# Second feed-forward stage: gate and up of two token blocks by seven half-depth products, the third block in a pass of its own

## The reference, cut to what matters

```python
def _rmsnorm(x, g):
    y = xf * lax.rsqrt(jnp.mean(xf * xf, axis=-1, keepdims=True) + EPS)
    return (y * g).astype(x.dtype)

def _swiglu(x, w_gate, w_up, w_down):
    return (jax.nn.silu(x @ w_gate) * (x @ w_up)) @ w_down

x = x + 0.5 * _swiglu(_rmsnorm(x, ffn1_norm[l]), ffn1_w_gate[l], ffn1_w_up[l], ffn1_w_down[l])
y, ... = _mixer(_rmsnorm(x, mix_norm[l]), ...)      # convolution and mLSTM, output projection
x = x + y
x = x + 0.5 * _swiglu(_rmsnorm(x, ffn2_norm[l]), ffn2_w_gate[l], ffn2_w_up[l], ffn2_w_down[l])
return _rmsnorm(x, final_norm)
```

## Time and profile before

| | us |
|---|---|
| median of 3 runs | 1892.54 |
| lowest, highest | 1892.49, 1892.79 |
| the profiled execution | 1891.52 |
| its span on the chip | 1889.8 |
| TensorE busy in the span | 1869.8 |
| VectorE busy | 881.0 |
| ScalarE busy | 498.2 |
| GpSimd busy | 97.7 |

### The profile page before, as it was taken

One profiled execution on the slowest core, in us unless ns is written; L12 is line 12 of the kernel. 1 busy time (PEld: TensorE's weight loads), 2 busy tenths in 40 slices (PEclk: granted clock), 3 DMA queues, 4 the chain that ended last, 5 costly groups with the idle time before them and its releaser, 6 DMA issues.

```text
span 1889.8 us, 31119 instructions
## 1 busy us (share of the span) xinstructions
PE 1869.8 (99%) x12577; PEld 1855.6 (98%) x12577; DVE 881.0 (47%) x1536; ACT 498.2 (26%) x883; POOL 97.7 (5%) x156
## 2 busy tenths in 40 slices
PE   8999999999999999999999999999999999999998
PEld 8999999999999999999999999999999999999998
DVE  6524433443444338513688865534434443343344
ACT  5302211221122124334444633212211221122022
POOL 1000000000000013200110022000000000000001
PEclk9999999999999999999999999999999999999999
DMA  7012201220121012311111322012201210220102
GB/s 226 26 43 67 67 22 44 67 67 22 44 67 52 14 54 73 82 45 45 35 34 41 132 81 68 23 46 67 67 22 44 67 50 16 67 67 23 55 1 92
DMA packets 144178, 105.10 MB, mean 56 GB/s; under 512 B 6376, under 2 KB 136248, under 8 KB 144120
## 3 DMA queue, kind: packets, MB, share of 16 engines
q1 hardware_dynamic: 144032, 104.27, 18.0%
q10 hardware_dynamic: 88, 0.02, 0.0%
HBM read 95.36 MB, written 8.92 MB: 55 GB/s over the span
## 4 chain that ended last, share of the span: by engine, by line
PE 94%; DVE 4%; ACT 1%; issue 0%; DMA 0%; POOL 0%; DVEq 0%
PE bank L218 30%; PE bank L224 29%; PE bank L223 29%; PE bank L222 1%; PE bank L220 1%; PE bank L678 1%; PE bank L2105 0%; PE bank L2119 0%; PE bank L2118 0%; PE bank L2121 0%; PE bank L685 0%; PE bank L941 0%; ACT in_hi L1209 0%; PE bank L2148 0%; DVE ffn_normed L194 0%
## 5 line engine op out<-in xcount | busy, mean ns | idle before, releaser
L218 PE MATMUL bank<-in_hi,w_hi 128*128 128x352 f32 x2256 | 712.9, 316 | 3.4 <-DVE w_lo L1109 1.6
L223 PE MATMUL bank<-in_lo,w_hi 128*128 128x352 f32 x2256 | 705.0, 313 | 0.0
L224 PE MATMUL bank<-in_hi,w_lo 128*128 128x352 f32 x2256 | 705.0, 313 | 0.0
L218 PEld LDWEIGHTS bank<-in_hi,w_hi 128*128 128x128 f32 x2256 | 426.4, 189 | 6.7 <-issue 2.2
L223 PEld LDWEIGHTS bank<-in_lo,w_hi 128*128 128x128 f32 x2256 | 426.5, 189 | 1.2
L224 PEld LDWEIGHTS bank<-in_hi,w_lo 128*128 128x128 f32 x2256 | 426.4, 189 | 0.0
L423 DVE TENSOR_TENSOR ffn_hidden<-ffn_silu,bank 128x352 f32<-128x352 f32 x132 | 68.7, 521 | 595.8 <-PE bank L224 528.9
L218 PE MATMUL bank<-ffn_hidden_hi,ffn_w_hi_more 128*128 128x352 f32 x1056 | 331.0, 313 | 1.0 <-DVE x L434 1.0
L434 DVE SCALAR_TENSOR_TENSOR x<-bank,x 128x352 f32<-128x352 f32 x528 | 261.1, 524 | 127.3 <-PE bank L224 92.3
L223 PE MATMUL bank<-ffn_hidden_lo,ffn_w_hi_more 128*128 128x352 f32 x924 | 288.8, 313 | 0.0
L224 PE MATMUL bank<-ffn_hidden_hi,ffn_w_lo_more 128*128 128x352 f32 x924 | 288.8, 313 | 0.0
(11 more groups left out here) (224 smaller groups left out, 1480.9 us busy)
## 6 DMA issues: line engine op xcount, KB each, us to landing
raw<-in_ffn_w_gate SPq DMA_DIRECT2D x44, 512.0 KB, 4.0
ffn_raw_more<-in_ffn_w_down SPq DMA_DIRECT2D x44, 512.0 KB, 5.3
raw<-in_w_in SPq DMA_DIRECT2D x24, 512.0 KB, 3.9
raw<-in_ffn_w_up SPq DMA_DIRECT2D x22, 512.0 KB, 5.0
ffn_raw_more<-in_ffn_w_up SPq DMA_DIRECT2D x22, 512.0 KB, 5.3
x_parked<-x SPq DMA_DIRECT2D x3, 1408.0 KB, 5.6
x<-x_parked SPq DMA_DIRECT2D x3, 1408.0 KB, 10.8
raw<-in_w_out SPq DMA_DIRECT2D x8, 512.0 KB, 4.9
```

What stands on the lines that cost most here:

```text
L218: pe.matmul(out, w_hi, in_hi, start=first, stop=False)
L223: pe.matmul(out, w_hi, in_lo, start=False, stop=False)
L224: return pe.matmul(out, w_lo, in_hi, start=False, stop=last)
```

## The change

The hidden stage is taken out of `ffn_phase` for the second feed-forward and rewritten as `last_ffn_phase`:

- Blocks 0 and 1 are done first, for all 11 pairs. The first two pairs are done as before (four plain rounds). For the nine pairs after that, gate and up of two tiles and two blocks are one product of 2x2 half matrices (two output tiles by two halves of the depth, and two halves of the depth by two blocks), made from seven products of half depth (12 matmuls each: four parts of 128, three products) instead of eight. Sums and differences of weight halves (t) are made on VectorE from the raw tiles and split on ScalarE and VectorE; sums and differences of the inputs (s1 to s4) are made once, in the plain rounds and behind them. The results are summed on VectorE while further products accumulate in the same banks. Down is done as before, for two blocks in one go, 96 matmuls.
- Block 2 has its place in `in_hi`/`in_lo` taken by s1 and s2 in the meantime. Its norm split is made at the end of the ninth such pair, and it goes through the 11 pairs alone in a third pass, for which all weight tiles are loaded and split a second time. The down tiles are loaded into the raw buffers of gate.
- The final norm's transposes of tiles 0 to 4 stand in the last three rounds; its output buffers are nine, each used once.
- The two feed-forward stages share the weight semaphores, so the counts of the second have an offset `base`.

The core of the diff:

```diff
+PRODUCTS = ("x11", "s2", "s1", "s3", "x12", "x22", "s4")
+DOWN_RAW = {**SLOT, ("down", 0): SLOT["gate", 0], ("down", 1): SLOT["gate", 1]}
+    # SyncE
+        def pair_loads(pair, number, seven, next_tile, last):
+            if not (isinstance(number, int) and number == 0):
+                sp.wait_ge(f.low["gate"], number * 2 + (base * 2 + 2))
+                if seven:
+                    sp.wait_ge(q.t_made, kind_index(pair, "gate") * 4 + 4)
+                load("down", pair, DOWN_RAW)
...
+                sp.wait_ge(f.low["down"], number * 2 + (base * 2 + 2))
...
+            load("gate", next_tile, SLOT)
+            sp.wait_ge(f.low["up"], number * 2 + (base * 2 + 2))
+            if seven:
+                sp.wait_ge(q.t_made, kind_index(pair, "up") * 4 + 4)
+            load("up", next_tile, SLOT)
+    # VectorE: sums of the inputs
+        def sums(k, n):
...
+            whole(f0, x21)
+            whole(f1, inputs["x22"][k])
+            step_op(f1, f0, f1, ALU.add)
+            whole(f0, inputs["x11"][k])
+            step_op(f2, f1, f0, ALU.subtract)
+            whole(f3, inputs["x12"][k])
+            step_op(f3, f3, f2, ALU.subtract)
+            s_low("s1", k, f1, n)
+            s_low("s2", k, f2, n + 1)
+            s_low("s4", k, f3, n + 2)
+        def third_sums():
+            for k in range(HALF):
+                whole(f0, (sh.in_hi[:, k, block_columns(1)], sh.in_lo[:, k, block_columns(1)]))
+                whole(f2, inputs["x11"][k])
+                step_op(f2, f2, f0, ALU.subtract)
+                s_low("s3", k, f2, 12 + k)
+    # VectorE: the plain rounds
+                hidden_of(step, 0, silu_four)
...
+                if (pair, b) == (0, 1):
+                    sums(0, 0)
+                if (pair, b) == (1, 0):
+                    sums(2, 6)
+                if b:
+                    weight_low(dve, sh, f, "gate", 0, pair + 1)
+                    weight_low(dve, sh, f, "up", 0, pair + 1)
+                hidden_of(step, 1, silu_four)
...
+                for d in range(4, KT):
+                    add(r * 8, b, d, down_bank)
+                    if (pair, b) == (1, 1) and d == 4:
+                        t_low(0, 0)
+                        t_make("gate", 1, 0)
+                if (pair, b) == (0, 1):
+                    sums(1, 3)
+                if (pair, b) == (1, 0):
+                    sums(3, 9)
+                if (pair, b) == (1, 1):
+                    t_low(2, 0)
+                    t_low(1, 0)
+                    t_make("gate", 3, 0)
+                    third_sums()
+    # VectorE: a pair of the seven products
+            a16("gate", kg, silu_four)
+            t_low(3, kg)
+            t_make("up", 0, ku)
+            t_make("up", 2, ku)
+            weight_low(dve, sh, f, "down", 0, pair, DOWN_RAW)
+            weight_low(dve, sh, f, "down", 1, pair, DOWN_RAW)
+            both22("gate", kg, silu_four)
+            t_low(0, ku)
+            t_make("up", 1, ku)
+            t_low(2, ku)
+            c21("gate", kg, silu_four)
+            t_low(1, ku)
+            t_make("up", 3, ku)
+            c12("gate", kg, silu_four)
+            a16("up", ku, hidden)
+            t_low(3, ku)
+            weight_low(dve, sh, f, "gate", 0, pair + 1)
+            weight_low(dve, sh, f, "gate", 1, pair + 1)
+            if not last:
+                t_make("gate", 0, ku + 1)
+                t_make("gate", 2, ku + 1)
+            both22("up", ku, hidden)
+            hidden_make(0)
+            if not last:
+                t_low(0, ku + 1)
+            hidden_make(1)
+            low(0)
+            if not last:
+                t_make("gate", 1, ku + 1)
+                t_low(2, ku + 1)
+            low(1)
+            c21("up", ku, hidden)
+            hidden_make(2)
+            low(2)
+            c12("up", ku, hidden)
+            hidden_make(3)
+            if not last:
+                t_low(1, ku + 1)
+            low(3)
+            if not last:
+                t_make("gate", 3, ku + 1)
+            own_adds_done(pair * 16)
...
+            if last:
+                weight_low(dve, sh, f, "up", 0, pair + 1)
+                adds(range(2))
+                weight_low(dve, sh, f, "up", 1, pair + 1)
+                adds(range(2, 4))
+                norm_split_dve(dve, sh, own_norm, gain, lambda k: adds(range(4 + k, 5 + k)))
+                adds(range(12, 16))
+            else:
+                adds(range(4))
+                weight_low(dve, sh, f, "up", 0, pair + 1)
+                adds(range(4, 6))
+                weight_low(dve, sh, f, "up", 1, pair + 1)
+                adds(range(6, 16))
+    # TensorE: a pair of the seven products
+                for name in PRODUCTS:
+                    if name == "s2":
+                        pe.wait_ge(q.t_low, kind * 4 + T_SPLIT[1])
+                        if w == "gate":
+                            pe.wait_ge(s.x_added, count - 1)
+                            if first:
+                                pe.wait_ge(q.s_step, S_EARLY_STEPS)
+                    if name == "s1" and w == "gate":
+                        pe.wait_ge(s.x_added, count)
+                    if name == "s3":
+                        if first and w == "gate":
+                            pe.wait_ge(q.s_step, S_STEPS)
+                        pe.wait_ge(q.summed, kind * 5 + 1)
+                    if name == "x12":
+                        pe.wait_ge(q.first_copied, kind + 1)
+                    if name == "x22":
+                        pe.wait_ge(q.summed, kind * 5 + 2)
+                        pe.wait_ge(q.t_low, kind * 4 + 4)
+                    if name == "s4":
+                        pe.wait_ge(q.summed, kind * 5 + 3)
...
+            drain(down(count, tiles, ((1, 0), (0, 2)), seven_down, pair, True))
+            drain(down(count + KT, tiles, ((0, 1), (1, 3)), seven_down, pair, False))
+    # third pass, VectorE
+            for j in range(2):
+                weight_low(dve, sh, f, "down", j, number, DOWN_RAW)
+            hidden_of(step, 0, last_silu)
+            tail.scales(dve, tiles)
+            if not last:
+                weight_low(dve, sh, f, "gate", 0, number + 1)
+                weight_low(dve, sh, f, "up", 0, number + 1)
+            hidden_of(step, 1, last_silu)
```

More of the change, by code:

```diff
@@ L210, in norm_split_act, with products @@
                        ).then_inc(sh.norm_high, 1)
-def products(pe, out, w_hi, w_lo, in_hi, in_lo, first=True, last=True, low_ready=None):
+def products(pe, out, w_hi, w_lo, in_hi, in_lo, first=True, last=True, low_ready=None, resumed=False):
     in_hi, in_lo = streamed(in_hi), streamed(in_lo)
+    if resumed:
+        pe.matmul(out, w_hi, in_hi, start=False, stop=False, skip_group_check=True)
+        pe.matmul(out, w_hi, in_lo, start=False, stop=False, skip_group_check=True)
+        return pe.matmul(out, w_lo, in_hi, start=False, stop=last, skip_group_check=True)
     pe.matmul(out, w_hi, in_hi, start=first, stop=False)
@@ L914, in final_norm @@
     banks = [(bank[a], bank[b]) for a, b in
-             ((4, 5), (6, 7), (6, 7), (4, 5), (0, 2), (0, 2), (1, 3), (4, 5), (6, 7))]
-    SLOTS = 6
-    out = [sh.raw[t % SLOTS] for t in range(TILES)]
-    x_done = [(FT // 2 * BLOCKS - BLOCKS + b + 1) * KT for b in range(BLOCKS)]
+             ((4, 5), (6, 7), (4, 5), (6, 7), (4, 5), (0, 2), (1, 3), (4, 5), (6, 7))]
+    out = [*(sh.x[:, KT + t, 0:D_MODEL] for t in range(4)), *(sh.raw[i] for i in (4, 5, 3, 0, 1))]
+    x_done = [FT // 2 * 2 * KT, FT // 2 * 2 * KT, FT // 2 * BLOCKS * KT]
     gain_in = sh.sem("y_gain_in")
@@ L925, in final_norm @@
     scaled = sh.sem("y_scaled")
-    stored = [sh.sem(f"y_stored{i}") for i in range(SLOTS)]
+    stored = sh.sem("y_stored")
     block = sh.block
@@ L985, in both, with act_round @@
         square(act, t, 1)
-    def act_round(act, b, hidden):
-        if b == 1:
-            hidden(0, lambda: both(act, 0))
-            both(act, 1)
-            hidden(1, None)
-        else:
-            hidden(0, lambda: both(act, 2))
-            both(act, 3)
-            hidden(1, lambda: both(act, 4))
+    def act_round(act, tiles, hidden, rest):
+        hidden(0, lambda: both(act, tiles[0]))
+        if len(tiles) > 1:
+            both(act, tiles[1])
+        rest()
+        hidden(1, None)
     def act_end(act):
@@ L1021, in scale, with scales @@
                                      gain[0:n, cols], ALU.mult, ALU.mult).then_inc(scaled, 1)
-    def dve_round(dve, b, hidden):
-        hidden(0)
-        if b == 1:
-            scale(dve, 0)
-            scale(dve, 1)
-            hidden(1)
-        else:
-            scale(dve, 2)
-            scale(dve, 3)
-            hidden(1)
-            scale(dve, 4)
+    def scales(dve, tiles):
+        for t in tiles:
+            scale(dve, t)
     def dve_end(dve):
@@ L2350, in encoder_kernel @@
             with ExitStack() as hidden_ctx:
-                hidden2 = hidden_buffers(nc, "ffn2", hidden_ctx)
```

(2 more changed lines are left out.)

550 lines of the change are left out of this document (515 added, 35 removed).

## The result

The changed kernel takes 1919.6 us (median of 4 runs, 1916.9 to 1920.0) against 1892.7 (1892.5 to 1894.2) before: a ratio of 1.0138, 95% interval 1.012 to 1.0155. Slower by 27 us, with 216 matmuls fewer. The profiled execution is 1919.3 around a span of 1917.6 us.

A forecast was written before the change was run, and what follows sets the result against it. TensorE, busy 99% of 1889.8 us, was taken as the bound; +2.1 +0.9 +13.5 +1.4 +2.4 +2.6 +8.0 = +30.9 on 1891.5 gave 1922.4, as a median about 1923.5 us; range with 8 in 10: 1898 to 1939.

The forecast's parts named there:

- the third pass: Block 2's rounds alone: late loads delay the second hidden product 1.15 us a round in seven rounds, +8.0 us.
- The steady pair: Seven-product pairs: VectorE's queue makes the first add 1.6 us late; period 43.26 against 42.96, eight times, +2.4 us.
- walk: Step-by-step timing of the engines' queues through rounds, seam, pair and third pass, using operation durations from profile rows.
- The seam: From fourth plain round into the seven products: waits of 3.1 and 8.2 us on VectorE, +13.5 us.
- The clock: After TensorE's 8 us stand at the seam, s3 and x12 at half rate: 0 to 3.6 us, taken as +1.4.
- the 24 matmuls that I priced: s3 and x12 behind the seam's wait, taking 3.6 us more at half rate, 2.2 of it under x22's wait.
- The plain rounds: Input sums on VectorE delay the second hidden product: +2.1 us in the second round, +0.9 in the third.
- my bounds of 0 to 2.3 a round: Limits on the third pass's delay per round, taken as 1.15 us; 0 if loads are 1.2 us faster.
- The sign named for this term: In the changed profile's last stage, seven TensorE waits of about 0.7 us on hidden_hi.

The follow-up runs named there:

- experiment 2: The changed kernel with the first two adds to x moved right behind the fourth hidden product in each pair of the seven products: 1906.21 us.
- experiment 4: The changed kernel with a pair's whole VectorE and ScalarE order set by when TensorE needs each result, same instructions: 1895.56 us.
- experiment 5: The kernel of experiment 4 with the first two adds moved ahead of one weight difference and the fourth hidden low part: 1892.98 us.
- Experiment 1: The changed kernel without the third input sums and their splits, so s3 multiplies what happens to lie there: 1908.98 us.
- experiment 7: The changed kernel with input sums' low parts behind the adds in plain rounds, and third-pass loads ordered gate 0, up 0, gate 1, up 1: 1915.67 us.
- experiment 9: Experiment 8's kernel with ScalarE's sum high parts behind the second hidden tile, ninth-pair adds spread over the norm, two fourth-round adds earlier: 1879.05 us.
- experiment 6: The changed kernel with only the way into the seven products reordered: alternating scratch tiles, some third sums and weight differences earlier: 1912.89 us.
- experiment 8: The edits of experiment 5, experiment 6 and experiment 7 together in one kernel: 1882.16 us, ratio 0.9944 to the kernel before the change.
- experiment 3: The changed kernel with the sums of both half products (both22) one operation earlier in gate and in up: 1913.72 us.

## Why the prediction held, and where it was off

The sign, the time (1923.5 forecast, 1919.6 measured) and the main mechanism held: the 3.6 us that a pair saves TensorE are spent waiting for VectorE, because the seven products need results back inside the pair. That the total came within 3.9 us is partly luck: the third pass was put 6.1 us too high, and 2.7 us before the stage were in no term.

- **The steady pair** came out as walked: 14.68 us from a16 to the first add (walk 14.65), period 43.25 (43.26). VectorE's queue has two gaps in between, 0.26 and 0.59 us, both for a high part that ScalarE makes and both in the walk. (The pair's VectorE operations add up to 31.7 us, not 31.8.) Experiments 2, 4 and 5 show that this is order, not capacity: the same work in order of due times takes 40.12. What cost the time was three operations (experiment 2: 1.8 us a pair) and more of the kind ahead of results that were due.
- **The seam** likewise: waits of 3.00 and 7.83 (3.1 and 8.2), first a16 at 39.0 (38.8). Experiment 1 puts 8.0 us of waiting on the third sums.
- **The clock**: 0.5 paid instead of 1.4. The lower clock on s2 lies under the wait for s3. Behind s3 it covers less than the 24 matmuls that I priced: the row of 1275 to 1280 (last section) has 18 matmuls in 4.51 us, where 30 fit at the high level, 1.8 us and not 3.6. x22 begins 6.12 us behind the first a16 (1274.82) and 5.52 behind it in a steady pair, so 0.6 of the 1.8 show there; the rest lies under the wait that x22 has in any pair.
- **The plain rounds**: +2.3 and +1.6 against +2.1 and +0.9. I walked VectorE and gave ScalarE none of its own queue; experiments 7 and 9 show that the high parts of the sums stood ahead of the SiLU.
- **The third pass was the term mis-sized: +1.9 instead of +8.0.** The step that failed is that the down loads "land 4.0 and 5.3 after their issue", and with it up 0 "at 13.5". Those durations came from a burst of four loads. Two down loads alone land sooner. Issue on SP's queue, and ScalarE's start on them (released by each landing), in the changed kernel:
```profile
1769.51 0.88 SPq L280 DMA_DIRECT2D raw<-in_ffn_w_down  x2
```
```profile
1773.13 1.06 ACT L289 ACTIVATE ffn_w_hi_more<-raw 128x1024 fp32r<-128x1024 f32 x1 [5.08 <-DMA raw<-in_ffn_w_down]
1774.43 1.06 ACT L289 ACTIVATE ffn_w_hi_more<-raw 128x1024 fp32r<-128x1024 f32 x1 [0.24 <-DMA raw<-in_ffn_w_down]
```
ScalarE is released 3.6 us behind the first issue and 4.9 behind it for the second, some 4.4 behind its own. In the round shown in experiment 7 the gate loads went out 4.9 us into the round instead of 5.9. From there the burst ran as read: ScalarE starts on up 0 7.7 us later (7.6 in the walk), and up 0's low part was done at 15.0 instead of 15.8. The hidden product ran at 14.87, 0.3 us later than in the kernel before (14.58), where my walk had 1.2. A slip of the walk itself adds to it: in a round of 22.6 us a load issued at 20.5 that takes 5.3 is in at 3.2 of the next, not 3.4, which is 1.4 of the 8.0. An estimate at the edge of slack turns an error of 1 us into seven times as much; my bounds of 0 to 2.3 a round held it. The sign named for this term, seven waits of about 0.7 on hidden's high part, did not show: the list has none in the third pass.
- **Missing: +2.7 before the stage.** The plan of the code there is unchanged; the granted clock isn't. (The low level is 1.2 GHz, the high one 2.4: the window's figure is a share of the high one.) The same three windows of the mixer, before and after (PEclk third from the right):
```profile
860.00:865.00 5.00, 5.00 (x52) 4.78 (x51) 1.63 (x4) 1.41 (x2) 0.00 (x0) 1.00 0.09 17
865.00:870.00 5.00, 5.00 (x41) 4.77 (x41) 0.89 (x3) 1.61 (x6) 1.42 (x3) 1.00 0.31 93
880.00:885.00 5.00, 5.00 (x36) 5.00 (x35) 1.64 (x7) 4.79 (x13) 0.00 (x0) 1.00 0.18 51
```
```profile
860.00:865.00 5.00, 5.00 (x40) 4.98 (x40) 1.63 (x4) 1.09 (x2) 0.00 (x0) 0.77 0.21 50
865.00:870.00 5.00, 5.00 (x38) 4.77 (x38) 0.89 (x3) 1.61 (x6) 0.47 (x2) 0.89 0.20 60
880.00:885.00 5.00, 5.00 (x24) 5.00 (x24) 2.43 (x9) 3.79 (x11) 0.00 (x0) 0.68 0.36 102
```
Each low stretch covers some 12 matmuls at 0.29 us a turn and costs 1.7 us; the changed kernel was 0.7 ahead when the first began (the small matmuls that it begins at 859.57 begin at 860.24 before). Both follow the mixer's small matmuls, with TensorE hardly pausing: the first begins at 862.7, the second at 879.8.
```profile
859.57 1.72 PE L2750 MATMUL bank<-ident,mix_rows 4*32 4x4 f32 x27
861.16 0.59 PE L2753 MATMUL bank<-mix_decay_row,pair_rows 4*128 4x9 f32 x4
...
878.42 1.14 PE L2801 MATMUL bank<-mix_values,mix_keys 32*128 32x258 f32 x4
```
The kernel before runs the same small matmuls at the same place and keeps 1.00, so they alone don't settle it. The stretches come and go between programs and executions: both in experiments 2 and 4, the first alone in 1, 6, 8 and 9, the second alone in 5, none in 3 and 7. What sets them off stays open; it wasn't tried.

## What to carry to other kernels

A form with fewer products pays only for what the helper engines return in time: walk one period of the helper's queue from the result that opens it to the result that TensorE is due, and put every operation that nobody waits for yet behind it; here this alone was worth 26.6 us (experiments 4 and 5 together). A side engine at 58% can be the bound when its order is wrong, and where two engines hand a value to and fro both queues must be moved (experiments 7 and 9). Sum waits only along one chain, and for a term that repeats, take its durations from a row in the same traffic.

## What the runs showed of the hardware

Behind a pause of 3.00 us of TensorE the changed kernel has the low level (1.2 GHz): the window grants 0.52, and the matmul takes 0.66 us.
```profile
1260.00:1262.00 2.00, 0.00 (x0) 0.00 (x0) 2.00 (x5) 0.34 (x1) 0.00 (x0) 1.00 0.03 8
1262.00:1264.00 2.00, 1.77 (x6) 1.77 (x7) 1.90 (x5) 0.00 (x0) 0.00 (x0) 0.52 0.00 0
...
1275.00:1280.00 5.00, 4.51 (x18) 4.54 (x19) 4.94 (x7) 3.15 (x5) 0.00 (x0) 0.59 0.00 0
```
The same pause of 2.99 us in experiment 1 cost nothing: the matmul took 0.42 and the window grants 1.00. And after 3.90 us the first matmul took 0.39 in experiment 8 with 0.57 from 1268 us on, and 0.63 in experiment 6. Shorter pauses can be followed by it too: the wait of 1.76 us in the second plain round left the clock at 1.00 in the changed kernel, but in experiments 3, 4 and 6 a low stretch begins within 1.6 us behind it, and the round took 25.45 us instead of 23.78. In experiment 1 the first matmul after the 1.76 us at the start of the third pass took 0.59 us, and that round 23.27 instead of 21.59. The windows, of experiment 3 and then of experiment 1:
```profile
1205.00:1210.00 5.00, 4.88 (x20) 4.62 (x21) 4.39 (x7) 1.96 (x3) 0.00 (x0) 0.66 0.10 16
1650.00:1655.00 5.00, 3.40 (x12) 3.40 (x13) 4.25 (x7) 1.98 (x2) 0.00 (x0) 0.67 0.00 0
```
So a wait of 1.8 to 3.9 us costs its clock or doesn't, some 1.7 us where it does, and an estimate should carry both ends. The Trainium skill ("TensorE: Matmul & The Clock Gate", part 1) has 1.2 GHz as the level of an idle array; the 0.52 behind the pause in the changed kernel agrees, and the 1.00 behind the same pause in experiment 1 shows that the length of the pause alone doesn't decide.

VectorE's operations took 0.52 us on 352 columns, 0.69 on 512 and 1.22 to 1.23 on 1024. The Trainium skill ("VectorE: DVE Perf Modes", the section on the TRN2 errata) gives (N + 151)/0.96 ns for an fp32 tensor_tensor, which is 0.52, 0.69 and 1.22: the traces agree, as does the one row of 512 columns that the prediction had (692 ns).
